# Two of four weight-block sums by adding transfers, ScalarE's copies earlier at one chunk, norm's sums before the next rounding

## The reference

```python
def _rmsnorm(x, g):
    xf = x.astype(jnp.float32)
    y = xf * lax.rsqrt(jnp.mean(xf * xf, axis=-1, keepdims=True) + EPS)
    return (y * g.astype(jnp.float32)).astype(x.dtype)

def _swiglu(h, w_gate_up, w_down):
    gu = h @ w_gate_up
    gate, up = gu[..., :D_FF], gu[..., D_FF:]
    return (jax.nn.silu(gate) * up) @ w_down

def sqrelu_mlp(xn, w1, w2):
    return jnp.square(jax.nn.relu(xn @ w1)) @ w2
# in each layer: h = h + mixer(rmsnorm(h)); h = h + ffn(rmsnorm(h))
```

## Time and profile before

| | before |
|---|---|
| median of 3 runs | 2227.39 us |
| the profiled execution | 2226.88 us |
| its span | 2224.7 us |
| TensorE busy | 2205.6 us (99%) |
| VectorE busy | 1624.4 us (73%) |
| ScalarE busy | 1141.4 us (51%) |
| GpSimd busy | 0.2 us |
| DMA | 206.94 MB, mean 93 GB/s |

### The profile page before, as it was taken

The page is one execution under the profiler, slowest core; times in us unless marked ns, Lnnn a source line. Parts: engine busy times, 40 slices in busy tenths (PEclk is TensorE's granted clock), DMA queues, the critical chain, the costliest instruction groups (busy, mean ns, idle before and its releaser), DMA issues.

```text
span 2224.7 us, 32419 instructions
## 1 busy us (share of the span) xinstructions
PE 2205.6 (99%) x13130; PEld 1912.2 (86%) x13130; DVE 1624.4 (73%) x2428; ACT 1141.4 (51%) x1843; POOL 0.2 (0%) x4
## 2 busy tenths in 40 slices
PE   9999999999999999999999999999999999999999
PEld 7777899999778999998899888998987767898997
DVE  5755978787676969697777796676764777786674
ACT  5755644444475634355544563543555886543542
POOL 0000000000000000000000000000000000000000
PEclk9999999999999999999999999999999999999999
DMA  4222223232322223232321222223232112232222
GB/s 153 79 86 76 95 95 110 90 114 73 106 98 76 95 95 110 90 114 76 120 67 58 95 90 100 95 103 106 77 121 76 58 58 76 95 103 106 95 89 101
DMA packets 37300, 206.94 MB, mean 93 GB/s; under 512 B 4256, under 2 KB 4768, under 8 KB 17824
## 3 DMA queue, kind: packets, MB, share of 16 engines
q1 hardware_dynamic: 34560, 199.17, 25.9%
q10 hardware_dynamic: 2592, 5.70, 0.8%
HBM read 202.76 MB, written 2.10 MB: 92 GB/s over the span
## 4 chain that ended last, share of the span: by engine, by line
PE 90%; DVE 4%; ACT 3%; issue 1%; DMA 1%; SPq 0%; ACTq 0%; DVEq 0%
PE ps L981 30%; PE ps L346 17%; PE ps L348 17%; PE ps L347 17%; PE ps L1485 2%; ACT high_w L401 1%; DVE low_w L422 1%; PE ps L2685 1%; PE ps L1540 1%; PE ps L1509 1%; PE ps L2216 1%; PE ps L1535 1%; PE ps L2704 1%; PE ps L1501 1%; DVE form_sums_s L377 0%
## 5 line engine op out<-in xcount | busy, mean ns | idle before, releaser
L422 DVE TENSOR_TENSOR low_w<-raw_w,high_w 128x2048 fp32r<-128x2048 f32 (+4 forms) x211 | 420.3, 1993 | 101.7 <-ACT high_w L401 101.4
L401 ACT ACTIVATE high_w<-raw_w 128x2048 fp32r<-128x2048 f32 (+4 forms) x211 | 352.1, 1670 | 148.8 <-DMA raw_w<-in_w_m_dn 93.9
L346 PE MATMUL ps<-ffn_hidh,high_w 128*128 128x512 f32 x864 | 336.5, 390 | 0.0
L347 PE MATMUL ps<-ffn_hidl,high_w 128*128 128x512 f32 x864 | 336.3, 389 | 0.0
L348 PE MATMUL ps<-ffn_hidh,low_w 128*128 128x512 f32 x864 | 336.1, 389 | 0.0
L981 PE MATMUL ps<-forms_th,forms_s 128*128 128x256 f32 x816 | 231.7, 284 | 8.1 <-ACT forms_kept L1027 8.1
L981 PE MATMUL ps<-form_lows_t,forms_s 128*128 128x256 f32 x816 | 231.4, 284 | 0.0
L981 PE MATMUL ps<-forms_th,form_lows_s 128*128 128x256 f32 x816 | 231.4, 284 | 0.0
L981 PE MATMUL ps<-xh,high_w 128*128 128x256 f32 x816 | 231.2, 283 | 0.0
L981 PE MATMUL ps<-xl,high_w 128*128 128x256 f32 x816 | 231.1, 283 | 0.0
L981 PE MATMUL ps<-xh,low_w 128*128 128x256 f32 x816 | 231.1, 283 | 0.0
(11 more groups left out here) (347 smaller groups left out, 4553.2 us busy)
## 6 DMA issues: line engine op xcount, KB each, us to landing
raw_w<-in_w_f_gu SPq DMA_DIRECT2D x44, 1024.0 KB, 4.8
raw_w<-in_w_m_up SPq DMA_DIRECT2D x32, 1024.0 KB, 4.8
raw_w<-in_w_m_dn SPq DMA_DIRECT2D x24, 1024.0 KB, 4.8
raw_w<-in_w_f_dn SPq DMA_DIRECT2D x8, 1024.0 KB, 4.8
raw_w<-in_w_m_dn SPq DMA_DIRECT2D x16, 512.0 KB, 3.4
raw_w<-in_w_b_qk SPq DMA_DIRECT2D x8, 1024.0 KB, 4.8
raw_w<-in_w_f_dn SPq DMA_DIRECT2D x8, 896.0 KB, 4.6
raw_w<-in_w_f_dn SPq DMA_DIRECT2D x16, 448.0 KB, 3.3
```

Of the source, the lines that this page charges most:

```text
L346: pe.matmul(out, sh, mh, start=start, stop=False)
L347: pe.matmul(out, sh, ml, start=False, stop=False)
L401: act.activation(wh[slot][:, 0:elems], raw[slot][:, 0:elems], ACT.Copy).then_inc(w_rounded, 1)
L422: dve.tensor_tensor(wl[slot][:, 0:elems], raw[slot][:, 0:elems], wh[slot][:, 0:elems].bitcast(F32), ALU.subtract).then_inc(w_split, 1)
```

## The change

**The sums.** L377 is gone from VectorE. For each formed chunk SyncE issues, behind the load of its weights, a second transfer from memory (`base_sums`): block A21 twice, into S3 and S1 (512 KB). It carries the wait for the fourth product of chunk f-2. GpSimd, which now has a program of its own (`add_sums`), waits for this transfer and issues a third one, which adds A11 and A22 from memory to S3 and S1 (`accum_op=ALU.add`, 512 KB more). VectorE waits for that one (`form_added`) before it makes S2 and S2 + A12 as before.

**The copies.** In the first formed chunk of each layer (`n == U.plain`) ScalarE now takes copies 1 and 2 ahead of the rounding of the next chunk's weights and ahead of the activation of the chunk before; only the sums are rounded earlier (`round_sums(c + 2)` in the last plain chunk).

**The norm's sums.** In the last chunk of a down stage which is followed by a norm without formed chunks, `sums_high` and `sums_low` come ahead of the rounding and the split of chunk c+2. The other cases are as before.

Two semaphores of a half chunk are shared with another pair instead of being new ones.

```diff
+    s_based = [Mark(x_loaded[i], 16) for i in range(2)]
+    s_added = [sem(f"form_added{i}") for i in range(2)]
+    def base_sums(sp, c):
+
+        f = FORM_OF[c]
+        if f >= 2:
+            sp.wait_ge(Z["product"], 6 * (f - 2) + 4)
+        sp.dma_start(s_raw[f % 2][:, S3:S1 + 1, :], blocks_of(c)[:, A21:A21 + 1, :].broadcast_to([P, 2, 512]))\
+          .then_inc(s_based[f % 2].sem, 16)
+
+    def add_sums(pool):
+
+        for c, f in FORM_OF.items():
+            wait_for(pool, s_based[f % 2], 16 * (f // 2 + 1))
+            pool.dma_start(s_raw[f % 2][:, S3:S1 + 1, :], blocks_of(c)[:, A11:A22 + 1:2, :], accum_op=ALU.add)\
+                .then_inc(s_added[f % 2], 16)
...
             dve.wait_ge(w_loaded[slot], 16 * (c // NS + 1))
-            if f >= 2:
-                dve.wait_ge(Z["product"], 6 * (f - 2) + 4)
-            dve.tensor_tensor(to[:, S3:S1 + 1, :], w[:, A11:A22 + 1:2, :],
-                              w[:, A21:A21 + 1, :].broadcast_to([P, 2, 512]), ALU.add).then_inc(Z["summed"], 1)
-            dve.wait_ge(Z["summed"], 3 * f + 1)
+            dve.wait_ge(s_added[f % 2], 16 * (f // 2 + 1))
...
@@ resid_act @@
             if F:
                 fold_act(act, F, n)
+            if F and n == end and not F.inner and not forms:
+                sums_high(act, F)
             round_weights(act, c + 2)
-            if F and n == end and not F.inner:
+            if forms and n == end:
                 sums_high(act, F)
...
@@ resid_dve @@
             fold_dve(dve, F, n)
+            if n == end and not F.inner and not forms:
+                sums_low(dve, F)
             split_weights(dve, c + 2)
-            if n == end and not F.inner:
+            if n == end and forms:
                 sums_low(dve, F)
...
@@ up_act, one(c, n) @@
+                if n < U.plain - 1:
+                    round_weights(act, c + 2)
+                else:
+                    round_sums(act, c + 2)
+            elif n and n == U.plain:
+                keep(act, U, c, 0)
+                keep(act, U, c, 1)
+                round_weights(act, c + 1)
+                keep(act, U, c, 2)
+                keep(act, U, c, 3)
+                if U.swiglu:
+                    silu(n - 1)
+                    rounded(n - 1)
+                else:
+                    square(n - 1)
+                    for j in range(2):
+                        rounded(n - 1, j)
+                    act.wait_ge(Z["product"], 6 * U.form(n) + 5)
+                    act.activation(sq[:, 0, 0:HT], ps[:, 2 * U.pair(c), 0:HT], ACT.Relu).then_inc(Z["read"], 1)
                 round_weights(act, c + 2)
...
@@ sync, load_w(c) @@
             sp.dma_start(raw[c % NS][:, 0:elems], array[at]).then_inc(w_loaded[c % NS], 16)
+            if c in FORM_OF:
+                base_sums(sp, c)
...
+    @block.gpsimd
+    def _(pool):
+        add_sums(pool)
```

More of the change, by code:

```diff
@@ L363, in four, with blocks_of @@
         return x[:, 0:SLOT].rearrange("p (b n) -> p b n", b=4)
+    s_based = [Mark(x_loaded[i], 16) for i in range(2)]
+    s_added = [sem(f"form_added{i}") for i in range(2)]
+    def blocks_of(c):
+        array, _, at = CHUNKS[c]
+        return array[at].rearrange("p (b n) -> p b n", b=4)
+    def base_sums(sp, c):
[9 more added lines that the diff above has]
+                .then_inc(s_added[f % 2], 16)
     def sum_weights(dve, upto):
@@ L374, in sum_weights @@
             dve.wait_ge(w_loaded[slot], 16 * (c // NS + 1))
-            if f >= 2:
-                dve.wait_ge(Z["product"], 6 * (f - 2) + 4)
-            dve.tensor_tensor(to[:, S3:S1 + 1, :], w[:, A11:A22 + 1:2, :],
-                              w[:, A21:A21 + 1, :].broadcast_to([P, 2, 512]), ALU.add).then_inc(Z["summed"], 1)
-            dve.wait_ge(Z["summed"], 3 * f + 1)
+            dve.wait_ge(s_added[f % 2], 16 * (f // 2 + 1))
             dve.tensor_tensor(to[:, S2, :], to[:, S1, :], w[:, A11, :], ALU.add).then_inc(Z["summed"], 1)
-            dve.wait_ge(Z["summed"], 3 * f + 2)
+            dve.wait_ge(Z["summed"], 2 * f + 1)
             dve.tensor_tensor(w[:, A21, :], to[:, S2, :], w[:, A12, :], ALU.add).then_inc(Z["summed"], 1)
@@ L389, in round_sums @@
                 f = FORM_OF[c]
-                act.wait_ge(Z["summed"], 3 * f + 2)
+                act.wait_ge(Z["summed"], 2 * f + 1)
                 act.activation(s_hi[f % 2][:, :, :], s_raw[f % 2][:, :, :], ACT.Copy).then_inc(Z["rounded"], 1)
@@ L399, in round_weights @@
             if c in FORM_OF:
-                act.wait_ge(Z["summed"], 3 * FORM_OF[c] + 3)
+                act.wait_ge(Z["summed"], 2 * FORM_OF[c] + 2)
             act.activation(wh[slot][:, 0:elems], raw[slot][:, 0:elems], ACT.Copy).then_inc(w_rounded, 1)
@@ L411, in split_sums @@
             dve.wait_ge(Z["rounded"], f + 1)
-            dve.wait_ge(Z["summed"], 3 * f + 3)
+            dve.wait_ge(Z["summed"], 2 * f + 2)
             dve.tensor_tensor(s_lo[f % 2][:, :, :], s_raw[f % 2][:, :, :], s_hi[f % 2][:, :, :].bitcast(F32),
@@ L466, in split_second @@
         prepared["dve"] = 1 + n
-    out_half_rounded = sem("out_half_rounded")
-    out_half_split = sem("out_half_split")
+    out_half_rounded = Mark(w_half_rounded, 1)
+    out_half_split = Mark(w_half_split, 1)
     def round_half(act, c, n):
@@ L475, in round_half @@
         act.activation(wh[slot][:, HALF[n]], raw[slot][:, HALF[n]], ACT.Copy)\
-           .then_inc(w_rounded if n else out_half_rounded, 1)
+           .then_inc(w_rounded if n else out_half_rounded.sem, 1)
         prepared["act"] = c + n
@@ L483, in split_half_weights @@
         else:
-            dve.wait_ge(out_half_rounded, 1)
+            wait_for(dve, out_half_rounded, 1)
         dve.tensor_tensor(wl[slot][:, HALF[n]], raw[slot][:, HALF[n]], wh[slot][:, HALF[n]].bitcast(F32),
-                          ALU.subtract).then_inc(w_split if n else out_half_split, 1)
+                          ALU.subtract).then_inc(w_split if n else out_half_split.sem, 1)
         prepared["dve"] = c + n
```

## The result

The changed kernel takes 2743.6 us, median of four runs (2739.3 to 2748.6), against 2227.0: the ratio is 1.232, with a 95% interval of 1.230 to 1.234. It is slower by 516.6 us. The prediction was 2506 with a range from 2370 to 2680. The direction and the place were right, the size was not, and the time lies above the range.

A forecast was written before the change was run, and what follows sets the result against it. TensorE, busy 2205.6 of 2224.7 us, was taken as the bound. Links 248.5 + entries 17 - 8.1 - 1.7 - 0.8 for the moves + clock 24 = +279 us on 2226.9, giving 2506 (range 2370 to 2680).

The forecast's parts named there:

- The mechanism: In seven-product runs, product 4 waits for ScalarE's first copy, queued behind sums made by two serial transfers; some 6 us each.
- The room of 1.87 us: Slack between successive product 4s in SwiGLU runs: sum, rounding and copy fill 8.2 of 10.08 us.
- The count of 40 links: Product-4-to-product-4 loops, from each run's third formed chunk: 28 in SwiGLU layers, 12 in MLPs; together +248.5 us.
- ScalarE's copies and the norm's sums: Reorderings at each layer's first formed chunk and the norm: waits -8.1, clock -1.7, norm's sum -0.8 us.
- the price of the second transfer: GpSimd's 512 KB add in each link: 5.8 us, between 4.8 for 1024 KB and 6.8 for two passes.
- The slow rival: GpSimd's add takes 8.5 us, with the clock falling at every stall: +445 us, 2672; chance 0.27.
- first transfer: SyncE's copy of A21 twice into the sums' buffer, 512 KB: 3.4 us from issue to landing.
- GpSimd's wait and issue: Between the two transfers in each link, GpSimd's wait for the first: 0.1 us.
- product 4, above the sum's 1.44 and 0.1: Product 4 takes 1.44 us plus 0.1 handing over; half speed adds 1.2, half taken over 40 stalls: +24 us.
- entries: Starts of ten runs following a down stage: product 4 late by 1.4 us in eight, 2.8 in two; +17 us.
- gains of the two moves: Copies first and norm's sums first remove TensorE waits and a clock fall: -10.6 us.
- half of 48 us: Clock falls behind the 40 new stalls, making product 4 run at half speed: +24 us, bounds 0 and 48.

The follow-up runs named there:

- e8: Changed kernel without the second, adding transfer (S3 and S1 are A21 alone): 2280 us.
- e3: Changed kernel with transfers only for the first two formed chunks of each run, VectorE adding S3 and S1 from the third on: 2275.6 us.
- e6: Changed kernel, but within the runs the next weights' load waits until the adding transfer has landed: 2660 us.
- e2: Changed kernel with GpSimd's second transfer copying A11 and A22 over S3 and S1, nothing added: 2596 us.
- e1: Changed kernel with S3 and S1 added by VectorE again, no transfers into the sums' buffer, both reorderings kept: 2218.1 us, 0.996 of before.
- e5: Changed kernel with the second transfer a plain copy without adding, issued by SyncE behind its wait for the first: 2518 us.
- e4: Changed kernel plus 72 unused matmuls ahead of the wait for the first copy in the 40 middle chunks of the runs: 2620 us.
- e9: Changed kernel with an adding transfer of half the size, only A22 added to S1 (256 KB), S3 left as A21: 2612.5 us.

## Why the prediction was wrong in size

**Right.** The mechanism, step by step: the wait that passed from L377 to SyncE's transfer, the two transfers in series, the queue on ScalarE, and TensorE's product 4 behind the first copy. The room of 1.87 us: the wait in e8 shows it to the tenth. The count of 40 links: e8 has 40 waits, and e3, which takes out just these, loses 468 us. ScalarE's copies and the norm's sums: forecast -10.6, measured -8.7.

**The step that failed** is the price of the second transfer, "the middle of 4.8 and 6.8, 5.8 us". It takes 8.7 as the mean of the 40 links (7.2 to 10.2). Two things went into that, and the runs give each. The add by itself takes 6.6 us (e6): 2.4 more than the 4.2 of GpSimd's copy, near my two passes of 6.8, and 0.8 above the price that I took. The load of the next weights goes out with it and adds 2.1 (e6). In the forecast I had put this at nothing, and it stood in the order on SyncE's queue: I had written that its next load needs chunk c finished, and not that chunk c finishes when the second transfer starts. So the larger part of the error is a transfer beside it, and not what adding costs. The slow rival had the right reason ("now three are under way per chunk"), but its 8.5 was a 1 MB load's time; that the number fits an add of 512 KB so well is luck. The Trainium skill (DMA: Bandwidth & Descriptors, "Anatomy of one DMA — SWDGE (gpsimd) path") gives about 2.0 us plus bytes over 436 GB/s for a transfer, an estimate of 3.2 us here. The traces disagree: the copy from GpSimd takes 4.2 us with no load issued near it (5.9 as the median in e2's issue table), and the add without company 6.6.

The whole of the miss, 2743.6 - 2506 = 238 us, term by term, with 40 links:

| term | forecast | measured | difference |
|---|---|---|---|
| second transfer | 5.8 us | 8.7 us | 2.9 x 40 = 116 |
| first transfer | 3.4 us | 4.4 us | 1.0 x 40 = 40 |
| GpSimd's wait and issue | 0.1 us | 0.3 us | 0.2 x 40 = 8 |
| product 4, above the sum's 1.44 and 0.1 | 0.6 us | 1.5 us | 0.9 x 40 = 36 |
| entries (e3 less e1) | 17 us | 57.5 us | 40 |
| gains of the two moves | -10.6 us | -8.7 us | 2 |

The differences add up to 242, 4 more than the miss. **The slow rival** had the add at 8.5 and came to 2672. It lacks the first transfer and GpSimd's wait (48 us), 0.2 us of the add (8), 0.3 us per link at product 4 (12), and 8 us at the entries and in the gains: 2748.

**The clock.** I took half of 48 us because four waits had brought one fall. Those were of 1.7 to 2.4 us. The waits of 7.9 to 11.8 us in the changed kernel's 40 links brought a fall in each, and so did those of 4.3 us and more in e5's; waits of 1.25 us (e8) or filled ones (e4) bring none. The price at product 4 was right (1.2 forecast, 1.24 measured), the frequency was not. The other 0.2 to 0.3 us in the table's row is mostly the way the rows are read (see e8).

**The entries** cost 57.5 and not 17 us. I had reckoned the copy late in ten of them by 1.4 or 2.8 us, 1.7 on average, and in e3 they wait 3.0. The same too low price of the second transfer, 6.6 us there and not 5.8, is 0.8 of that 1.3. The rest of the 40 us is spread: four shorter waits for ScalarE at the other runs, 3.5 us of waits for the weights' split, about 9 us of product 4 at half speed (0.992 as the mean clock), and some 10 us that I have not placed.

**Open.** Why the first transfer lands in 3.25 us in e4's links and in 4.3 in the others, why the add at the entries is 1 us faster in e4, and what makes up the second half of the 1.0 us by which the first transfer was too cheap.

## What to carry to other kernels

Before you move work from a half-idle engine to transfers, find out whether it stands in a loop: if what it makes is in place of something that TensorE has just freed, its latency counts in full, and 1.2 us of VectorE are cheaper than 13 us of two transfers in series, however idle the queues are. The room of the link, read from three rows of the timeline, says how much latency it bears (here 1.87 us), and the number of links multiplies every error in the price of one. A transfer that the trace doesn't show is priced with what goes out beside it. When two runs differ in the time of a transfer, compare the order of issue too, before the difference is put down to the engine that issues.

## What the runs showed of the hardware

- 512 KB from memory to SBUF with no load issued just before: 4.3 us from SyncE (e5), 4.2 as a copy from GpSimd (e2, first two chunks of the runs), 6.6 as an add from GpSimd (e6). With a 1 MB load issued at about the same time: 5.9 as the copy from GpSimd (e2), 8.7 as the add. The add of 256 KB: 4.2 without, 6.0 with (e9).
- The load makes GpSimd's transfer start later and not run slower: the add's first packet comes 4.0 us behind its issue instead of 1.8.
- On GpSimd's queue an add goes in twice as many packets as a copy of the same bytes (18496 against 9792) and takes about twice the engines' time. The count alone is not the price: SyncE's copy in e5 adds 18496 packets to its queue too (71552 against 53056), and takes 4.3 us.
- Behind waits of 4.3 us and more in the links (e5, changed kernel) TensorE ran product 4 at half speed in all 80 cases: 2.7 us from its first matmul to the one behind its twelve, against 1.53 behind waits of 1.25 us (e8) and 1.44 in the stream.
- Filling the wait with matmuls whose results nobody uses gave back 123 of 517 us; the waits are better removed.
